# Making the coefficients of a gathered expert layer on ScalarE, and dividing the gather buffers six and six

## What is computed

```python
def chunk(hx):                                   # PEER: 8 heads, top 16 each
    q = ...                                      # queries, 8 heads x 2 halves of 128
    s = jnp.einsum('bthpc,hpnc->bthpn', q, sub_keys)
    top_s, top_i = lax.top_k(s, PEER_TOPK)       # 16 of 128 in each half
    cand_s = top_s[..., 0, :, None] + top_s[..., 1, None, :]
    best_s, best_pos = lax.top_k(cand_s.reshape(...), PEER_TOPK)
    expert = jnp.take_along_axis(cand_i, best_pos, axis=-1)
    gate = jax.nn.softmax(best_s, axis=-1)
    u_sel = jnp.take(u, expert, axis=0)
    v_sel = jnp.take(v, expert, axis=0)
    act = jax.nn.gelu(jnp.einsum('btd,bthkd->bthk', hx, u_sel), approximate=False)
    return jnp.einsum('bthk,bthkd->btd', (gate * act).astype(h.dtype), v_sel)
```

## Time and profile before

| | before |
|---|---|
| median of 3 runs | 2486.46 us (2483.32 to 2488.86) |
| the profiled execution | 2487.36 us, span 2485.6 us |
| TensorE busy (matmul) | 1982.1 us, 80% |
| VectorE busy | 1413.1 us, 57% |
| ScalarE busy | 576.7 us, 23% |
| GpSimd busy | 1027.1 us, 41% |
| gathers (queue q0) | 553.72 MB, 59.6% of the 16 DMA engines' span |
| granted TensorE clock, mean | 0.927 |

### The profile page before, as it was taken

The page is one execution under the profiler, slowest core; times in us unless marked ns, Lnnn a source line. Parts: engine busy times, 40 slices in busy tenths (PEclk is TensorE's granted clock), DMA queues, the critical chain, the costliest instruction groups (busy, mean ns, idle before and its releaser), DMA issues.

```text
span 2485.6 us, 21257 instructions
## 1 busy us (share of the span) xinstructions
PE 1982.1 (80%) x6918; PEld 1101.4 (44%) x6918; DVE 1413.1 (57%) x3068; ACT 576.7 (23%) x1204; POOL 1027.1 (41%) x1063
## 2 busy tenths in 40 slices
PE   6756767767898789768877887688877799897998
PEld 3641222222333335423344463243322297676996
DVE  0138788755344554694455447855555455555884
ACT  1111100100112431011134211111100134453663
POOL 0025656766444454464444545656666400000000
PEclk9888989999998889999988899999999899998999
DMA  3257989999889789989966899999999744353653
GB/s 146 85 168 309 371 314 367 369 368 356 320 301 345 272 285 393 348 305 357 396 235 234 329 385 346 343 370 409 396 364 368 284 144 154 111 153 103 187 182 122
DMA packets 194843, 707.96 MB, mean 285 GB/s; under 512 B 21784, under 2 KB 23072, under 8 KB 194480
## 3 DMA queue, kind: packets, MB, share of 16 engines
q0 software_dynamic: 152064, 553.72, 59.6%
q1 hardware_dynamic: 40960, 150.65, 17.9%
q10 hardware_dynamic: 1712, 2.24, 0.3%
HBM read 704.81 MB, written 1.06 MB: 284 GB/s over the span
## 4 chain that ended last, share of the span: by engine, by line
PE 54%; DVE 17%; issue 10%; DMA 7%; POOL 6%; ACT 3%; another core or an unknown queue 1%; ACTq 0%; SPq 0%; DVEq 0%; POOLq 0%
PE ps L494 22%; PE ps L652 15%; DMA a<-in_peer_u,eidx 7%; PE ps L411 5%; PE ps L426 5%; DVE a L1435 4%; POOL a L349 3%; POOL a L344 3%; DVE diag L1444 1%; DVE a L1369 1%; PE ps L444 1%; PE ps L397 1%; PE ps L598 1%; DVE a L1375 1%
## 5 line engine op out<-in xcount | busy, mean ns | idle before, releaser
L494 PE MATMUL ps<-a,diag 128*128 128x512 f32 (+1 forms) x2112 | 1091.9, 657 | 356.2 <-DVE diag L1444 237.2
L494 PEld LDWEIGHTS ps<-a,diag 128*128 128x128 f32 (+1 forms) x2112 | 402.9, 203 | 994.2 <-issue 623.0
L1435 DVE SCALAR_TENSOR_TENSOR a<-a,ps 128x1024 f32<-128x1024 f32 x512 | 622.3, 1216 | 347.3 <-DMA a<-in_peer_u,eidx 289.3
L344 POOL DMA_INDIRECT a<-in_peer_u,eidx x528 | 522.5, 990 | 636.7 <-DVE a L1435 303.4
L349 POOL DMA_INDIRECT a<-in_peer_v,eidx x528 | 503.8, 954 | 303.3 <-issue 133.3
L652 PE MATMUL ps<-a_r 128*128 128x256 f32 (+1 forms) x1648 | 393.8, 332 | 19.9 <-DVE a_r L1583 7.3
L932 ACT ACTIVATE gel<-dots 128x1 f32<-128x1 f32 x528 | 101.1, 201 | 1076.6 <-DVE a L1435 637.9
L652 PEld LDWEIGHTS ps<-a_r 128*128 128x128 f32 x1648 | 279.6, 192 | 52.3 <-DVE a_r L1583 8.1
L1577 DVE TENSOR_TENSOR ring_r<-wring,a_r 128x1024 fp32r<-128x1024 f32 x142 | 173.3, 1222 | 139.8 <-ACT a_r L1091 139.7
L1444 DVE TENSOR_SCALAR diag<-cstc,gel,a 128x128 f32<-128x128 f32 (+1 forms) x528 | 186.1, 354 | 104.0 <-issue 38.9
L1091 ACT ACTIVATE a_r<-wring 128x1024 fp32r<-128x1024 f32 x142 | 149.4, 1053 | 82.3 <-PE ps L652 82.2
(11 more groups left out here) (218 smaller groups left out, 1299.1 us busy)
## 6 DMA issues: line engine op xcount, KB each, us to landing
wring<-in_units SPq DMA_DIRECT2D x270, 512.0 KB
a<-in_peer_u,eidx POOLq DMA_INDIRECT x528
a<-in_peer_v,eidx POOLq DMA_INDIRECT x528
cs2c<-in_cs SPq DMA_DIRECT2D x1, 1792.0 KB
a<-in_poolm SPq DMA_DIRECT2D x1, 1632.0 KB, 9.2
h<-in_xin SPq DMA_DIRECT2D x2, 512.0 KB, 4.2
bcF<-in_bc_rows SPq DMA_DIRECT2D x2, 512.0 KB, 9.3
a<-in_mem SPq DMA_DIRECT2D x1, 1024.0 KB, 4.9
```

Source lines behind the costliest of these rows:

```text
L344: g.indirect_dma_start(ug[:, n % NU, :], None, peer_u, bass.IndirectOffsetOnAxis(ap=eidx[:, t, k:k + 1], axis=0))\
L494: last = nc.tensor.matmul(ps[0:P, 6 + j, :], diag[:, k % 4, 0:P], vg[:, k % NV, j * 512:(j + 1) * 512], start=False, stop=False)
L1435: v.scalar_tensor_tensor(ug[:, n % NU, :], ug[:, n % NU, :], 1.0, hnm if t == 2 else ps2(4), ALU.mult, ALU.mult, accum_out=dots[:, k % 8:k ...
```

## The change

`gelu` on ScalarE becomes `coef`: Gelu, then gate times Gelu into a new column buffer `cgt` (a Copy with a pointer scale), then identity times that column into `diag` (a Copy of 128x128, or of 128x16 for tile 2, with a pointer scale). Each waits for the one before, and the last also for the matmuls of four slots back. Since gates are now read by another engine, the last step of `topk` signals `gates`, and ScalarE waits for it at the first slot of a tile (and in layer 0, tile 0, at slot 64). VectorE's `coef`, its place two slots behind, and `flush` go; its slot is a dot alone. TensorE's LAG is 1. NU and NV are 6 and 6, and the `vg` buffer goes by `n` and not by `k`, as 6 divides neither 16 nor 128.

```diff
-NU = 4
-NV = 8
+NU = 6
+NV = 6
...
-LAG = 2
+LAG = 1
...
+        cgt = sb("cgt", [128, 8])
...
-                pe.wait_ge(S(f"v{k % NV}"), vfill)
+                pe.wait_ge(S(f"v{n % NV}"), vfill)
...
-            def gelu(k, n):
+            def coef(t, k, n):
+
+                unit_mat, W = (cc("sel", 16), 16) if t == 2 else (ident, 128)
+                c = slice(k % 8, k % 8 + 1)
+                if k == 0 or (n, k) == (16 + SLOTS // 2, SLOTS // 2):
+                    l = 0 if n < 16 + 2 * SLOTS else 1
+                    act.wait_ge(S("gates"), tk_number(l, t, 1 if k else 0))
                 act.wait_ge(S("dot"), n + 1)
-                nc.scalar.activation(gel[:, k % 8:k % 8 + 1], dots[:, k % 8:k % 8 + 1], ACT.Gelu)\
-                    .then_inc(S("gelu"), 1)
-
-            def beside(base):
-                return Beside(lambda k: gelu(k, base + k))
+                nc.scalar.activation(gel[:, c], dots[:, c], ACT.Gelu).then_inc(S("gelu"), 1)
+                act.wait_ge(S("gelu"), n + 1)
+                nc.scalar.activation(cgt[:, c], gel[:, c], ACT.Copy, scale=gates[t][:, k:k + 1]).then_inc(S("cg"), 1)
+                act.wait_ge(S("cg"), n + 1)
+                if n >= 4:
+                    act.wait_ge(S("vsum"), n - 3)
+                nc.scalar.activation(diag[:, k % 4, 0:W], unit_mat, ACT.Copy, scale=cgt[:, c]).then_inc(S("diag"), 1)
+
+            def beside(t, base):
+                return Beside(lambda k: coef(t, k, base + k))
...
-                link(v.tensor_tensor(G3, G3, gs[:, h0:h0 + H].unsqueeze(2).to_broadcast([128, H, 16]), ALU.mult))
+                v.tensor_tensor(G3, G3, gs[:, h0:h0 + H].unsqueeze(2).to_broadcast([128, H, 16]), ALU.mult)\
+                    .then_inc(S("gates"), 1)
...
-            def coef(t, k, n, gate):
-
-                unit_mat, W = (cc("sel", 16), 16) if t == 2 else (ident, 128)
-                dve.wait_ge(S("gelu"), n + 1)
-                if n >= 4:
-                    dve.wait_ge(S("vsum"), n - 3)
-                v.tensor_scalar(diag[:, k % 4, 0:W], unit_mat, gel[:, k % 8:k % 8 + 1], gate,
-                                ALU.mult, ALU.mult).then_inc(S("diag"), 1)
-
             def straight(t, base):
 
-                def slot(k):
-                    if k < SLOTS:
-                        dot(t, k, base + k)
-                    if k >= 2:
-                        coef(t, k - 2, base + k - 2, gates[t][:, k - 2:k - 1])
-                return slot
-
-            def flush(t, base, n):
-                for k in (n - 2, n - 1):
-                    coef(t, k, base + k, gates[t][:, k:k + 1])
+                return lambda k: dot(t, k, base + k)
```

More of the change, by code:

```diff
@@ L491, in sums_slot @@
                 pe.wait_ge(S("diag"), n + 1)
-                pe.wait_ge(S(f"v{k % NV}"), vfill)
+                pe.wait_ge(S(f"v{n % NV}"), vfill)
                 for j in range(2):
                     last = nc.tensor.matmul(ps[0:P, 6 + j, :], diag[:, k % 4, 0:P],
-                                            vg[:, k % NV, j * 512:(j + 1) * 512], start=False, stop=False)
+                                            vg[:, n % NV, j * 512:(j + 1) * 512], start=False, stop=False)
                 last.then_inc(S("vsum"), 1)
@@ L987, in _ @@
                     gate_exps(0, 0)
-                gelu(k, m_base + k)
+                coef(2, k, m_base + k)
             y_out(2, 1)
-            first = beside(a_base)
+            first = beside(0, a_base)
             first.to(TOPK_A)
@@ L1075, in stick @@
                 out_(7)
-            front(0, beside(b_base))
+            front(0, beside(1, b_base))
             x_row(0)
@@ L1080, in _ @@
             (_, a_base), (_, b_base) = gathers(1)
-            front(1, beside(a_base))
+            front(1, beside(0, a_base))
             x_row(1)
@@ L1096, in x_high @@
                                      xT[:, :, t * 128:(t + 1) * 128], ACT.Copy).then_inc(S("x_high"), 1)
-            bg = beside(b_base)
+            bg = beside(1, b_base)
             bg.to(SIDE["mem"])
@@ L1468, in _ @@
             topk(0, 0, lambda n: bg.to(min(16, 16 * n / HALF_GATE_AT)))
-            flush(2, m_base, 16)
             bg = Beside(straight(0, a_base))
@@ L1474, in _ @@
             bg.to(SLOTS)
-            flush(0, a_base, SLOTS)
             def heads_norm(tag, tiles):
@@ L1566, in _ @@
             front(0, Beside(straight(1, b_base)))
-            flush(1, b_base, SLOTS)
             (_, a_base), (_, b_base) = gathers(1)
             front(1, Beside(straight(0, a_base)))
-            flush(0, a_base, SLOTS)
             def w_low(n):
```

## The result

The changed kernel takes 2511.28 us (median of 4 runs, 2510.5 to 2515.2), the kernel before 2484.89 us beside it (4 runs, 2481.65 to 2488.86): a ratio of 1.0109, interval 1.0089 to 1.0128, 26 us slower. Run once more later it gave 1.0110 (1.0089 to 1.0131). The forecast was 2471 us, faster.

The account below looks back on a forecast made before the run. It saw DMA bounding gather stretches, VectorE top-k, and a chain over several engines attention. Gains of 14, 4, 13, 6, 3, 6 and 3 us against a 34 us loss gave -15 us: 2471 us, range 2440 to 2507.

Parts of the forecast that it names:

- attention ticks: 16 head pairs of attention: one diagonal in stock instead of two, TensorE waits longer; loss 34 us (0 to 76).
- Top-k of layer 1: Two top-k stages bound by VectorE, which loses 7 us of coefficient work in each; gain 14 us (6 to 20).
- Starts of stages: Starts of k, v and q: one more diagonal in stock shortens TensorE's waits; gain 13 us (6 to 17).
- Meta slots: 16 slots before the second part of the indices, 0.25 us of VectorE work saved each; gain 4 us (0 to 5).
- first tile's end: End of the first tile: last slot no longer waits 3.04 us for its diagonal; gain 6 us (0 to 8).
- very end and last tile: Fewer slots left after the last dot, 3 us (1.7 to 4); rest of the last tile, 3 us (0 to 8).
- Six V buffers instead of eight cost nothing: Gathers: V is freed sooner, leaving 12.8 us for a transfer beside 13.4; six U buffers gain 6 us (0 to 12).
- Rival 1: Attention ticks: longer waits put the following bursts wholly at the low clock, adding 44 us: 2515 us; chance 0.19.
- Waits added: ScalarE waits for the matmul of four slots back before each diagonal, other work queued behind; nothing, bound 30 us.
- Rival 2: ScalarE's queue: evictions behind the diagonals come late, 30 us, 2501 us; chance 0.07.
- 1.05 MB costs 2.8 us whatever the engines do: Gather-only stretches: DMA busy 0.98 of the time at 371 GB/s sets 2.8 us a slot.
- Rival 4: Gathers at a DMA share of 0.98: deeper queue moves no more, 12 us of gains go, some 2484 us; chance 0.13.

Follow-up runs that it names:

- e2: Changed kernel with four U and eight V buffers, TensorE two slots behind and 16 places for dots, so only the coefficients move: 2466.9 us, 0.9936.
- r1: The changed kernel run again, nothing altered, on a slower chip: 2511.8 us, 1.0110 against the kernel before.
- r2: Kernel before with six U and six V buffers only, coefficients on VectorE, TensorE two slots behind, run a second time: 2509.3 us, 1.0107.
- e1: Kernel before with six U and six V buffers only, coefficients on VectorE, TensorE two slots behind, first run: 2516.8 us, 1.0124.
- e4: Changed kernel, six U and six V buffers, with TensorE two slots behind instead of one: 2478.4 us, 0.9974.
- e3: Changed kernel with four U and eight V buffers instead of six and six, TensorE still one slot behind: 2513.0 us, 1.0110.
- e7: Kernel before with gathers of 512 instead of 1024 values a row, dots multiplied by zero: 2481.4 us, 0.9980.
- e6: e2 with TensorE three slots behind instead of two: 2429.0 us, 0.9766.
- r4: e2 with TensorE four slots behind and eight places for diagonals: 2339.5 us where the kernel before takes 2425.9, 0.9644.

## Why the prediction was wrong, point by point

Two steps failed: six V buffers were said to cost nothing, and the moved coefficients were said to shorten stretches that they didn't shorten. A third, the attention ticks, had the mechanism right and the size too small.

- **Coefficient's price and Gelu to diagonal** (1.02 us): right, 0.96 us measured (the Gelu at 1044.18 us, its diagonal done at 1045.14).
- **Top-k of layer 1, -14 us:** right for the move alone (-6.1 and -5.6 in e2), and more than undone by the buffers in the changed kernel (+3.0 and +2.1 against before; +1.7 and +3.0 in r1).
- **Starts of stages, -13 us:** right, -13.6 us in e2 (158.1 to 148.3 us, 33.9 to 30.2, 104.1 to 104.0), though more of it in the first front and less in the second than the 7 and 6 forecast.
- **Meta slots -4, first tile's end -6, very end and last tile -6:** wrong: +3.6, -0.4 and -2.2 us in e2. The first is within what one kernel's traces differ by (63.3 us in the changed kernel, 60.0 in r1), so it shows no gain rather than a loss. In the last tile the gathers' issue and the interruptions set the time, not the coefficient; what sets the other two no run shows. With this the move is worth 19 us and not 43.
- **"Six V buffers instead of eight cost nothing":** this is the step that turned a gain of 6 into a loss. It compared times in a steady row (12.8 us beside 13.4) for transfers, and read the waits of the earlier trace rows as "U is the short side". But in the top-k stages slots come irregularly, and GpSimd's queue is one: a V gather that waits for TensorE stops the U gathers. The even buffers measured +12 us instead of -6 beside ScalarE's coefficients, +23 (r2) and +31 (e1) alone, all on the slower chips.
- **The attention ticks, +34 us:** mechanism right, size too small. The longest waits were 6.0 and 5.4 us for the 5.89 and 5.66 forecast, and in all the waits for diagonals grew from 26.7 to 41.8 and from 27.5 to 37.5 us, 25 us together. The two attentions grew by 45 us. The rest is the clock, 11 us (TensorE is busy 99.5 us instead of 96.0 and 139.2 instead of 131.8 for the same matmuls), which the prediction left to its bound, and, in the second front, some 10 us of other waits, most of them scores that wait for ScalarE behind late rises. That the distance costs 33 us by whole runs (after less e4), as forecast, is luck: the attentions alone grew by 43 there, and other stages gave 10 back.
- **Rival 1, the clock:** 2515 us, and 2511 were measured, but not for its reason. It priced the clock at 44 us more, where 11 came of it (14 between e2 and e3).
- **Waits added, 0 us:** about right. ScalarE's diagonals waited 44.6 us for TensorE in the changed kernel. In e2 they waited longer, 83 us and 102 more for a semaphore whose sender isn't recorded, and the kernel was still faster. Rival 2, with the rule of the Trainium skill ("ScalarE: Activation LUTs", Rules for kernel authors) that multiplications belong to VectorE, didn't occur: the move alone is 0.6% faster.
- **What bounds the gathering stretches:** "1.05 MB costs 2.8 us whatever the engines do" was wrong in its cause. Half the bytes cost the same on a slower chip, and on a quicker one a slot takes 2.56 us. Rival 4, with no deeper queue, named the right doubt and not the price.

Sum of the misses, by whole runs: 24 us of gains that weren't there, 18 us at the buffers, -1 at the distance, 41 us between -15 and +26. The forecast left out, too, that its own arithmetic of the ticks, read the other way, says that a deeper distance gains; that is worth more than all the rest.

Still open: what holds the rises back on one sort of chip, and how much of the even buffers' loss outside the second attention hangs on it.

## What to carry to other kernels

When one engine's work lies in a plan behind another's, price the distance by the stock it leaves at the places where the chain stops: here each slot of distance took 1.7 us off a wait and, in the second attention, the clock gave half as much again. The ratios run from 1.0110 at one slot to 0.9644 at four (the latter with eight places and on a quicker chip). A queue that serves two kinds of buffers in order is as deep as its scarcer kind at its latest moment, not on average. A DMA share near 1 doesn't prove that bytes are the bound; one run with half the bytes tells, for the chip that it runs on. And a stage's bytes, issue and waits can lie within a few per cent of one another, so that curing one of them gives next to nothing.

## What the runs showed of the hardware

- An indirect gather of 128 rows takes GpSimd some 0.94 us and 0.30 us to the next, whether a row has 4096 or 2048 bytes (the kernel before and e7).
- TensorE's rises of a semaphore reached ScalarE, VectorE and GpSimd late and in bunches of up to five, mostly after gaps of 4 us and more, on one sort of chip, and not on the other; the same kernel before takes 2.4% less there. On the first sort the rise behind the values' matmuls came 0.5 to 2.5 us late in the changed kernel's second attention, and 0.01 us behind them in e3's. The Trainium skill, "Perfetto Trace Analysis", Per-engine timelines, has the propagation of a semaphore as a part that the profile doesn't show; the rows above show that here it could be seen from what waited.
- With one, two, three and four slots in stock the granted clock of the first attention was 0.78, 0.86, 0.88 and 0.96, of the second 0.83, 0.90, 0.95 and 0.97 (e3, e2, e6, r4; r4 with eight places and on a quicker chip).
